# First norm applied behind the products, and four helper queues in another order, in a fused Trainium2 block kernel

## Chip, cores and metric

The kernel runs as one launch on one core of one Trainium2 chip. The metric is the device time of one launch in microseconds (us), the median over several runs; lower is better. The core has a matrix engine (TensorE, PE in the rows), a vector engine (VectorE, DVE), a scalar engine (ScalarE, ACT), GpSimd (POOL) and a queue of DMA issues on SyncE (SP); each works through its own instructions in the order written, and they wait for one another through semaphores only.

## The reference, cut to what matters

The whole network is computed for 256 tokens of width 1024: a gated linear recurrence layer, a key/value projection, a sliding-window attention layer, a feed-forward layer, a two-branch mixer, a second feed-forward layer and a final norm. The change touches the first layer and its surroundings:

```
h = rmsnorm(x, norm_g)                    # x * rsqrt(mean(x*x) + 1e-6) * g
u = h @ w_in                              # 1024 x 3072
xb, gate = u[..., :1536], u[..., 1536:]
xb = causal_depthwise_conv(xb, conv_w, conv_b)        # 4 taps over time
r = sigmoid(blocks(xb) @ wr + br)         # 16 blocks of 96
i = sigmoid(blocks(xb) @ wi + bi)
log_a = -8.0 * r * softplus(-lam)
a = exp(log_a)
b = sqrt(-expm1(2.0 * log_a)) * (i * xb)
hs = scan(a, b)                           # h[t] = a[t] h[t-1] + b[t]
x = x + (hs * silu(gate)) @ w_out
```

## The kernel before, in words

**Products.** Activations lie transposed, 128 channels on the partitions and 256 tokens along them, so the width 1024 is 8 tiles `k`. Each float32 product is made of three products of rounded parts: weight high part by activation high part, weight high by activation low, weight low by activation high (`passes`, L595). Weights come in chunks of 1 MB, each as two halves of 128x1024 numbers, into a double buffer `stage`. SP's queue issues the loads (L392); a load into a buffer waits until VectorE has finished with what lay in it. `hi(n)` on ScalarE rounds half `n` to `w_hi` (all ScalarE work is recorded at L1216), `lo(n)` on VectorE subtracts to give `w_lo` (L1729). Both go into a ring of four halves; PE frees a place (`ring_free`) when it has used a half. A half is 24 matmuls.

**First layer.** `a_w_in` is 12 chunks: `C_X` 0 to 5 give the convolved branch, `C_G` 6 to 11 the gate branch, one PSUM bank per chunk (256 channels by 256 tokens). Halves are numbered through all of them, with the block gates between: gate group g (0 to 3) has two smaller halves of 128x768, numbers 8 and 9, 12 and 13, 18 and 19, 22 and 23. Groups 0 and 1 follow chunks 3 and 4, groups 2 and 3 follow chunks 6 and 7. So halves 16 and 17 are chunk 6, 20 and 21 chunk 7, 24 and 25 chunk 8.

**What a convolved chunk c needs** when its products are done: `conv_b` (ScalarE, two instructions from the bank, last tap and bias), `conv` (VectorE, six `scalar_tensor_tensor`, the other three taps, bank and SBUF as sources, L1942), `xb_hi(c)` (ScalarE) and `xb_lo(c)` (VectorE, L1734). PE may write the bank of chunk c again when the convolution has read it (`conv_x`).

**What a gate group g needs**: its two halves; the convolved activations; and `stack(g)`, eight copies on POOL (L487) that gather the pieces of 96-wide blocks which straddle tiles. PE first runs 18 "main" matmuls, then 12 "rest" matmuls (L825 and L827) that read the stacked copies. Behind them ScalarE runs six tanh instructions, and `decay(g)` (six instructions, exponents); `decay` needs `lam_ready`, the last of some 15 tiny VectorE instructions (128x12) that compute softplus(-lam) by a series (L1883 to L1907). `lru_gated`, `lru_square`, `gate_out` and `decay_square` (POOL) follow.

**The start.** Both token halves of x are loaded, then chunk 0 of the weights. ScalarE and VectorE form the mean square of each token (squares summed along x), the root and its reciprocal; x is scaled by it (`rooted_x`, L1836), transposed a second time two tiles ahead of use (`turn_ahead`, L617), multiplied by the gain while it is split into `a_hi` (`normalised_hi`) and `a_lo` (L1841). Raw x is transposed too (L794) and copied to `xres` for the residual (`input_out`). `warm` (L783) are matmuls on constants ahead of the data.

**POOL's queue** holds, in this order: the gate weight pieces of groups 0 and 1 (L495, L503), those of groups 2 and 3, `stack(0)`, `stack(1)`, eight further pieces, 14 small loads for later layers (L507 to L519), `stack(2)`, a `decay_square`, `stack(3)`.

The order of work is written out by hand: each engine's program is a loop over the half number `n` with conditions in it. ScalarE's and VectorE's read, before:

```python
                if n - 1 in x_end:          # ScalarE
                    xb_hi(x_end[n - 1])
                if n not in x_end and n:
                    hi(n + 4)
                act.wait_ge(ring_free, n + 1)
                if n in x_end:
                    c = x_end[n]            # conv_b(c), then hi(n + 4)
```

## Time and profile before

| what | value |
|---|---|
| median of 3 runs | 785.8 us (785.65 to 786.15) |
| the profiled execution | 785.83 us |
| its span, first to last record | 783.9 us |
| PE busy | 775.7 us, 99% of the span, 5321 matmuls |
| VectorE busy | 585.7 us, 75% |
| ScalarE busy | 487.7 us, 62% |
| GpSimd busy | 107.1 us, 14% |

All rows come from the profiled execution. Starts are in us from the start of the span. In rows of a timeline the first number is the start, the second the time from the start of the first to the end of the last instruction of the row; in brackets stands how long the engine had been idle and for whom it waited. A row of one source line gives min/median/max duration in ns and the starts of the first and the last instruction. Instructions of one engine overlap a little, so the distance between two starts is shorter than a duration.

### The profile page before, as it was taken

How to read it: one execution, taken by the hardware profiler on the slowest of the kernel's cores; microseconds unless marked ns; L12 is line 12 of the kernel's file. 1: busy time of each engine (PE TensorE's matmuls, PEld its weight loads, DVE VectorE, ACT ScalarE, POOL GpSimd, SP SyncE). 2: the span in 40 equal slices, each digit the busy share in tenths (PEclk: the TensorE clock that was granted, in tenths of full speed). 3: DMA queues.
4: the chain of work that ended last, by engine and by line, in shares of the span. 5: the costliest groups of instructions: out<-in, count | busy, mean ns of one | idle time of the engine just before them, and what ended most of it. 6: DMA issues, size and time to landing. Idle time of an engine off the chain costs nothing.

```text
span 783.9 us, 14573 instructions
## 1 busy us (share of the span) xinstructions
PE 775.7 (99%) x5321; PEld 710.9 (91%) x5321; DVE 585.7 (75%) x892; ACT 487.7 (62%) x761; POOL 107.1 (14%) x195
## 2 busy tenths in 40 slices
PE   8999999999999999999999999999999999999997
PEld 7999999998998888888888899999999888888885
DVE  5998997978868887776459664796588887787443
ACT  7799947778675655554346565764656665555334
POOL 9697100157100000000000031000000000000000
PEclk9999999999999999999999999999999999999999
DMA  8663575634546766666665554445655676765651
GB/s 261 191 191 113 180 205 165 205 109 111 186 135 185 218 190 187 185 206 195 187 188 167 182 153 145 130 143 158 186 166 157 193 215 186 195 184 184 193 182 54
DMA packets 101557, 136.57 MB, mean 174 GB/s; under 512 B 5320, under 2 KB 86912, under 8 KB 101504
## 3 DMA queue, kind: packets, MB, share of 16 engines
q1 hardware_dynamic: 99232, 133.23, 56.4%
q0 software_dynamic: 2112, 2.54, 1.3%
q8 instruction: 35, 0.57, 0.3%
q14 instruction: 18, 0.15, 0.1%
q10 hardware_dynamic: 160, 0.07, 0.0%
HBM read 134.78 MB, written 1.05 MB: 173 GB/s over the span
## 4 chain that ended last, share of the span: by engine, by line
PE 96%; DVE 2%; ACT 1%; DMA 1%; issue 0%; SPq 0%; ACTq 0%
PE bank L595 34%; PE bank L658 21%; PE bank L660 11%; PE bank L603 8%; PE bank L704 8%; PE bank L751 5%; PE bank L752 3%; PE bank L945 1%; PE bank L927 1%; PE bank L952 1%; ACT acts L1216 1%; DMA arena<-x 1%; DVE w_lo L1729 1%; PE bank L955 0%; DVE acts L1767 0%; PE bank L827 0%
## 5 line engine op out<-in xcount | busy, mean ns | idle before, releaser
L1729 DVE TENSOR_TENSOR w_lo<-stage,w_hi 128x1024 fp32r<-128x1024 f32 x249 | 305.1, 1230 | 124.0 <-ACT w_hi L1216 123.4
L1216 ACT ACTIVATE w_hi<-stage 128x1024 fp32r<-128x1024 f32 (+1 forms) x251 | 262.4, 1051 | 117.6 <-PE bank L595 41.8
L595 PE MATMUL bank<-acts,w_hi 128*128 128x256 f32 x1520 | 277.3, 285 | 0.4 <-DVE acts L1841 0.3
L658 PE MATMUL bank<-acts,w_hi 128*128 128x512 f32 x704 | 244.8, 392 | 0.0
L595 PEld LDWEIGHTS bank<-acts,w_hi 128*128 128x128 f32 x1520 | 236.5, 192 | 2.7 <-issue 1.7
L595 PE MATMUL bank<-acts,w_lo 128*128 128x256 f32 x760 | 214.9, 283 | 0.0
L660 PE MATMUL bank<-acts,w_lo 128*128 128x256 f32 x704 | 197.2, 280 | 0.0
L658 PEld LDWEIGHTS bank<-acts,w_hi 128*128 128x128 f32 x704 | 131.7, 187 | 29.2
L595 PEld LDWEIGHTS bank<-acts,w_lo 128*128 128x128 f32 x760 | 145.7, 192 | 0.0
L660 PEld LDWEIGHTS bank<-acts,w_lo 128*128 128x128 f32 x704 | 133.1, 189 | 0.0
L1216 ACT ACTIVATE arena<-bank 128x512 f32<-128x512 f32 (+1 forms) x79 | 43.6, 561 | 63.7 <-PE bank L660 45.9
L603 PE MATMUL bank<-w_hi,acts 128*128 128x256 f32 (+1 forms) x320 | 71.8, 319 | 0.4 <-DVE w_lo L1729 0.4
L555 POOL TENSOR_SCALAR arena<-arena,rden 128x128 f32<-128x128 f32 (+1 forms) x44 | 23.4, 544 | 283.8 <-DVE rden L2108 283.2
L751 PE MATMUL bank<-acts,w_hi 128*128 (+1 forms) x176 | 61.1, 391 | 0.0
L1216 ACT ACTIVATE acts<-arena 128x512 fp32r<-128x512 f32 (+3 forms) x41 | 26.4, 644 | 52.7 <-DVE arena L2262 33.0
L1216 ACT ACTIVATE arena<-arena 128x512 f32<-128x512 f32 (+3 forms) x64 | 38.4, 605 | 29.7 <-DVE arena L2238 14.6
L603 PEld LDWEIGHTS bank<-w_hi,acts 128*128 128x128 f32 x320 | 52.2, 191 | 4.6 <-DVE w_lo L1729 0.8
L704 PE MATMUL bank<-w_hi,acts 128*128 128x512 f32 x176 | 54.4, 390 | 0.0
L603 PE MATMUL bank<-w_lo,acts 128*128 128x256 f32 (+1 forms) x160 | 50.5, 315 | 0.0
L752 PE MATMUL bank<-acts,w_lo 128*128 (+1 forms) x176 | 49.3, 280 | 0.0
L2230 DVE TENSOR_TENSOR arena<-arena,bank 128x512 f32<-128x512 f32 x44 | 30.2, 685 | 22.2 <-ACT arena L1216 22.2
L751 PEld LDWEIGHTS bank<-acts,w_hi 128*128 128x128 f32 x176 | 32.9, 187 | 7.2
(221 smaller groups left out, 809.4 us busy)
## 6 DMA issues: line engine op xcount, KB each, us to landing
stage<-ffn_w_gate SPq DMA_DIRECT2D x44, 512.0 KB, 4.3
stage<-ffn_w_up SPq DMA_DIRECT2D x44, 512.0 KB, 4.5
stage<-ffn_w_down SPq DMA_DIRECT2D x44, 512.0 KB, 3.6
stage<-w_in SPq DMA_DIRECT2D x40, 512.0 KB, 3.6
stage<-a_w_in SPq DMA_DIRECT2D x24, 512.0 KB, 4.5
stage<-b_w_in SPq DMA_DIRECT2D x16, 512.0 KB, 3.9
stage<-a_w_out SPq DMA_DIRECT2D x12, 512.0 KB, 3.7
stage<-b_w_out SPq DMA_DIRECT2D x8, 512.0 KB, 3.5
```

The source lines that it names most:

```text
L555: pool.tensor_scalar(s, s, rden[:, 2 * n + q:2 * n + q + 1], 1.0, ALU.mult, ALU.mult).then_inc(p_norm, 1)
L595: mm = pe.matmul(dst, w[:, slot, c:c + P], a[:, k, :] if isinstance(k, int) else a[:, bass.ds(k, 1), :], start=start and n == 0, stop=stop ...
L603: mm = pe.matmul(dst, a[:, k, tb * P:(tb + 1) * P], w[:, slot, c:c + n], start=start and i == 0, stop=stop and i == 2, skip_group_check=True)
L658: pe.matmul(two[p][:, m, :], w_hi[:, half % RING, c:c + P], wide(acts[:, k, :, :]), start=k == 0, stop=False, skip_group_check=True)
L660: mm = pe.matmul(two[p][:, m, 0:T], w_lo[:, half % RING, c:c + P], a_hi[:, k, :], start=False, stop=k == KD - 1, skip_group_check=True)
L704: mm = pe.matmul(token_bank(tb, h)[:, :], a[:, k, t], w[:, slot, c], start=False, stop=w is w_hi and a is a_hi, skip_group_check=True)
L751: pe.matmul(b[:, :], w_hi[:, half % RING, w], both, start=start, stop=False, skip_group_check=True)
L752: return pe.matmul(b[:, 0:T], w_lo[:, half % RING, w], high, start=False, stop=stop, skip_group_check=True)
L927: mm = pe.matmul(bank[score_bank(n + i)][:, c:c + w], q[r, t * T + c:t * T + c + P], k[r, 0:keys], start=True, stop=True)
L1216: return nc.scalar.activation(out_, in_, func, **kw)
L1729: dve.tensor_tensor(w_lo[:, n % RING, 0:w], src, w_hi[:, n % RING, 0:w].bitcast(F32), ALU.subtract)\
L2230: dve.tensor_tensor(y, y, two[ffn_two(n, j, u)][:, :, 0:T], ALU.add).then_inc(ff_add, 1)
```

## The change

1. x is loaded in halves of columns (channels 0 to 511, then 512 to 1023), with the first weight half between them. Raw x is transposed once, 16 transposes, into banks 0 to 3 and 6, 7 (`turned_x`); `a_hi` and `a_lo` are made from it with the gain alone. `rooted_x` and `turn_ahead` are gone. `WARM` goes from (8, 3) to (11, 2).
2. The squares are summed in four parts later on. The token factor is spread over the partitions by two matmuls inside chunk 1 (`first_roots`), copied to `spread`, and multiplied into each chunk's bank afterwards: `x_scale(c)` (VectorE, six times, result in SBUF at `x_unit`) for the convolved branch, and `gate_out(0..5)` for the gate branch, where 0 to 2 were plain copies before and 3 to 5 did not exist (`silu` read the bank).
3. `conv_b` and `conv` read `x_unit` in SBUF. PE waits for `x_scaled` of chunk c - 2 where it waited for `conv_x`. `gates(0)` waits for `x_ready` 4, now set by the last copy to `xres`, behind `conv_b(2)`.
4. ScalarE does `hi(n + 4)` ahead of `xb_hi` and ahead of `conv_b`; VectorE does `lo(n + 4)` ahead of `xb_lo` and ahead of `conv`.
5. The softplus series goes to POOL, ahead of `stack(0)`, 18 instructions in a chain (`decay_scale`); Abs and Exp stay on ScalarE, one sum and the reciprocal on VectorE.
6. Of the second pair's gate pieces 6 stay on POOL and 14 go to SP's queue, behind the loads of chunks 2, 3 and 4. The 14 small loads for later layers go from POOL to SP's queue, 11 behind the load of chunk 9 and 3 behind that of chunk 11.

```diff
-WARM = (8, 3)
+WARM = (11, 2)
...
-            for tb in range(TB):
-                sp.dma_start(x_tok[:, tb, :], xt[:, tb, :]).then_inc(x_in[tb], 16)
+            for j in range(2):
+                sp.dma_start(x_tok[:, :, 512 * j:512 * j + 512], xt[:, :, 512 * j:512 * j + 512]).then_inc(x_in[j], 16)
+                sp.dma_start(stage[:, 0, j, :].rearrange("p (b n) -> p b n", b=4), first[:, 4 * j:4 * j + 4, :])\
+                    .then_inc(stage_in[j], 16)
...
             for j in range(2, 6):
                 load(C_X + j, col(w_in, j), split(C_X + j - 2))
+                if j == 2:
+                    second_pieces()
+                elif j < 5:
+                    second_again(j - 3)
...
+            pieces(1, 0, 6)
+            decay_scale()
+            stack(0)
+            stack(1)
...
+            def first_roots():
+
+                pe.wait_ge(rstd_ready, 1)
+                pe.wait_ge(x_ready, 1)
                 for tb in range(TB):
-                    mm = pe.transpose(bank[5 + k % 3][:, tb * P:(tb + 1) * P], x_rst[:, tb, k * P:(k + 1) * P], ident)
-                mm.then_inc(xt_done, 1)
+                    mm = pe.matmul(bank[6][:, tb * P:(tb + 1) * P], n_rstd[:, tb:tb + 1].to_broadcast([P, P]),
+                                   ident, start=True, stop=True)
+                mm.then_inc(first_rb, 1)
...
                 if c >= 2:
-                    pe.wait_ge(conv_x, 2 * (c - 1))
-                col_chunk(C_X + c, 4 + c % 2, normed=0)
+                    pe.wait_ge(x_scaled, c - 1)
...
+                if n:
+                    hi(n + 4)
                 if n - 1 in x_end:
                     xb_hi(x_end[n - 1])
-                if n not in x_end and n:
-                    hi(n + 4)
                 act.wait_ge(ring_free, n + 1)
                 if n in x_end:
                     c = x_end[n]
-                    if c == 0:
-                        act.wait_ge(par_ready, 2)
+                    act.wait_ge(x_scaled, c + 1)
                     for m in range(2):
                         t = 2 * c + m
-                        f(tiles(XB + t), bank[4 + c % 2][:, m * T:(m + 1) * T], ACT.Identity,
+                        f(tiles(XB + t), x_unit(c)[:, m * T:(m + 1) * T], ACT.Identity,
...
                     if c == 0:
-                        input_out(2)
-                        input_out(3)
-                        hi(4)
-                    hi(n + 4)
+                        input_out(7)
+                    elif c < 3:
+                        input_out(2 * c - 2)
...
+            def x_scale(c):
+
+                dve.wait_ge(ring_free, half_of(C_X + c) + 2)
+                rooted(XU + 2 * (c % 2), 4 + c % 2).then_inc(x_scaled, 1)
...
                 if n - 1 in x_end:
+                    lo(n + 4)
                     xb_lo(x_end[n - 1])
...
                 if n in x_end:
                     c = x_end[n]
+                    x_scale(c)
...
+                    lo(n + 4)
...
-                            dve.scalar_tensor_tensor(x[:, tap:T], bank[4 + c % 2][:, m * T:(m + 1) * T - tap],
+                            dve.scalar_tensor_tensor(x[:, tap:T], x_unit(c)[:, m * T:(m + 1) * T - tap],
                                                      par_a[:, w:w + 1], x[:, tap:T], ALU.mult, ALU.add)\
```

How the queues change at three places.

VectorE around chunk 2 and gate group 0. `L1729` (now `L1823`) is `lo`, with `gate_st` of a gate group's half; `L1942` (now `L2022`) the convolution; `L1734` (now `L1828`) `xb_lo`; `L1913` `x_scale`. Before:

```order
L1734 TENSOR_TENSOR acts<-arena,acts 128x2x256 [waits xbh]
L1729 TENSOR_TENSOR w_lo<-gate_st,w_hi 128x768 [waits hi_done]
L1887 RECIPROCAL lam<-lam 128x12 [waits lam_step]
L1889 TENSOR_TENSOR lam<-lam 128x12 [waits lam_step]
L1942 SCALAR_TENSOR_TENSOR arena<-bank,par_a,arena 128x255 [waits conv_b]
L1942 SCALAR_TENSOR_TENSOR arena<-bank,par_a,arena 128x255
L1942 SCALAR_TENSOR_TENSOR arena<-bank,par_a,arena 128x254 [waits conv_s] x2
L1942 SCALAR_TENSOR_TENSOR arena<-bank,par_a,arena 128x253 [waits conv_s] x2
L1729 TENSOR_TENSOR w_lo<-gate_st,w_hi 128x768 [waits hi_done]
```

Now:

```order
L1823 TENSOR_TENSOR w_lo<-gate_st,w_hi 128x768 [waits hi_done]
L1828 TENSOR_TENSOR acts<-arena,acts 128x2x256 [waits xbh]
L1913 TENSOR_TENSOR arena<-bank,spread 128x512 [waits ring_free]
L1823 TENSOR_TENSOR w_lo<-gate_st,w_hi 128x768 [waits hi_done]
L2022 SCALAR_TENSOR_TENSOR arena<-arena,par_a 128x255 [waits conv_b]
L2022 SCALAR_TENSOR_TENSOR arena<-arena,par_a 128x255
L2022 SCALAR_TENSOR_TENSOR arena<-arena,par_a 128x254 [waits conv_s] x2
L2022 SCALAR_TENSOR_TENSOR arena<-arena,par_a 128x253 [waits conv_s] x2
```

Half 8 is now split ahead of `xb_lo(1)` and half 9 ahead of `conv(2)`, `x_scale(2)` stands between, and the convolution reads no bank.

ScalarE from gate group 1's tanh to gate group 2's halves. `lam` marks `decay`, `w_hi<-arena` the halves of group 2, `bank,par_a` with x5 tanh, two alone (or `arena,par_a` now) `conv_b`. Before:

```order
L1216 ACTIVATE arena<-bank,par_a 128x256 x5
L1216 ACTIVATE w_hi<-stage 128x1024 [waits ring_free,stage_in2]
L1216 ACTIVATE arena<-bank,par_a 128x256 [waits ring_free]
L1216 ACTIVATE arena<-bank,par_a 128x256
L1216 ACTIVATE w_hi<-stage 128x1024 [waits ring_free,stage_in3]
L1216 ACTIVATE arena<-arena,lam 128x256 [waits ri_sig,lam_ready]
L1216 ACTIVATE arena<-arena,lam 128x256 x5
L1216 ACTIVATE acts<-arena 128x2x256 [waits conv_x]
L1216 ACTIVATE w_hi<-stage 128x1024 [waits ring_free,stage_in0]
L1216 ACTIVATE w_hi<-stage 128x1024 [waits ring_free,stage_in1]
```

Now:

```order
L1304 ACTIVATE arena<-bank,par_a 128x256 x5
L1304 ACTIVATE w_hi<-stage 128x1024 [waits ring_free,stage_in2]
L1304 ACTIVATE w_hi<-stage 128x1024 [waits ring_free,stage_in3]
L1304 ACTIVATE arena<-arena,par_a 128x256 [waits x_scaled,ring_free]
L1304 ACTIVATE arena<-arena,par_a 128x256
L1304 ACTIVATE arena<-arena,lam 128x256 [waits ri_sig,lam_ready]
L1304 ACTIVATE arena<-arena,lam 128x256 x5
L1304 ACTIVATE w_hi<-stage 128x1024 [waits ring_free,stage_in0]
L1304 ACTIVATE acts<-arena 128x2x256 [waits conv_x]
L1304 ACTIVATE w_hi<-stage 128x1024 [waits ring_free,stage_in1]
```

Half 15 goes ahead of `conv_b(4)`, which now also waits for `x_scale(4)`; half 16 still stands behind `decay(0)` but ahead of `xb_hi(4)`.

POOL between its gate pieces and `stack(0)`. Before, `stack(0)` (L487) followed the last piece of gate_i:

```order
L495 DMA arena<-a_gate_i_w 64x2x96 x2
L495 DMA arena<-a_gate_i_w 32x2x96
L495 DMA arena<-a_gate_i_w 96x2x96
L487 CAST acts<-acts 32x256 [waits xbl]
L487 CAST acts<-acts 32x256 [waits stack_done] x3
L487 CAST acts<-acts 64x256 [waits stack_done] x4
```

Now the end of `decay_scale` stands there (an ISA row and the first 13 of its instructions are left out):

```order
L572 TENSOR_SCALAR lam<-lam 128x12 [waits lam_step]
L573 TENSOR_TENSOR lam<-lam 128x12 [waits lam_step]
L574 TENSOR_SCALAR lam<-lam 128x12 [waits lam_step]
L575 TENSOR_TENSOR lam<-lam 128x12 [waits lam_step]
L576 TENSOR_TENSOR lam<-lam 128x12 [waits lam_step]
L533 CAST acts<-acts 32x256 [waits xbl]
L533 CAST acts<-acts 32x256 [waits stack_done] x3
L533 CAST acts<-acts 64x256 [waits stack_done] x4
```

## Rows read from the trace of the kernel before

**Rows 1.** The page: busy time by engine.
```profile
PE 775.7 (99%) x5321; PEld 710.9 (91%) x5321; DVE 585.7 (75%) x892; ACT 487.7 (62%) x761; POOL 107.1 (14%) x195
```

**Rows 2.** Chain of waits that ended last, first 125 us: start, length, what.
```profile
9.96 0.98 PE bank L595 x6
...
17.91 19.66 PE bank L595 x162
37.57 0.12 PE bank L825
...
39.01 7.92 PE bank L595 x66
...
63.49 7.92 PE bank L595 x66
72.85 11.52 PE bank L595 x96
84.43 40.38 PE bank L595 x336
```

**Rows 3.** Timeline of PE and ScalarE, the start.
```profile
1.01 3.79 PE L783 MATMUL bank<-ones 128*128 128x128 f32 x16 [1.01 <-POOL half_pi L476]
5.23 1.97 PE L794 MATMUL bank<-con,arena 128*128 128x128 f32 x16
7.04 0.83 PE L783 MATMUL bank<-ones 128*128 128x128 f32 x6
7.79 0.63 ACT L1216 ACTIVATE w_hi<-stage 128x512 fp32r<-128x512 f32 x1 [0.40 <-DMA stage<-a_w_in]
17.63 0.25 PE L839 MATMUL bank<-con,rows_a 96*128 96x96 f32 x1
```

**Rows 4.** Line L775: a later norm's spread, the same form as `first_roots`.
```profile
L775 PE MATMUL bank<-con,n_rstd x8: 270/274/275, 145.8 to 425.9; 128*128 128x128 f32 x8
```

**Rows 5.** Timeline of VectorE, chunks 0 to 3.
```profile
19.48 2.42 DVE L1942 SCALAR_TENSOR_TENSOR arena<-bank,par_a,arena 128x255 f32<-128x255 f32 x6
21.82 2.35 DVE L1729 TENSOR_TENSOR w_lo<-stage,w_hi 128x1024 fp32r<-128x1024 f32 x2
24.08 0.68 DVE L1734 TENSOR_TENSOR acts<-arena,acts 128x512 fp32r<-128x512 f32 x1
30.79 0.95 DVE L1729 TENSOR_TENSOR w_lo<-gate_st,w_hi 128x768 fp32r<-128x768 f32 x1
31.66 0.22 DVE L1887 RECIPROCAL lam<-lam 128x12 f32<-128x12 f32 x1
```

**Rows 6.** Costliest groups by form: a bank times `spread`, in later norms.
```profile
L1819 DVE TENSOR_TENSOR arena<-bank,spread 128x512 f32<-128x512 f32 x14 | 9.6, 684 | 4.8 <-PE bank L595 4.8
```

**Rows 7.** Timeline of ScalarE, gate groups 1 and 2.
```profile
42.13 2.27 ACT L1216 ACTIVATE arena<-bank,par_a 128x256 f32<-128x256 f32 x6
44.27 1.09 ACT L1216 ACTIVATE w_hi<-stage 128x1024 fp32r<-128x1024 f32 x1
45.21 1.05 ACT L1216 ACTIVATE arena<-bank,par_a 128x256 f32<-128x256 f32 x2
46.11 1.10 ACT L1216 ACTIVATE w_hi<-stage 128x1024 fp32r<-128x1024 f32 x1
47.06 3.07 ACT L1216 ACTIVATE arena<-arena,lam 128x256 f32<-128x256 f32 x6
50.01 0.64 ACT L1216 ACTIVATE acts<-arena 128x512 fp32r<-128x512 f32 x1
```

**Rows 8.** Timeline of POOL: `stack(0)` and `stack(3)`.
```profile
30.94 5.13 POOL L487 CAST acts<-acts 32x256 fp32r<-32x256 f32 x8 [5.94 <-DVE acts L1734]
...
61.82 8.68 POOL L487 CAST acts<-acts 32x256 fp32r<-32x256 f32 x8 [0.68 <-POOL arena L525]
```

**Rows 9.** Line L487 on POOL at 32.2 to 33.5 (beside the convolution), then at 66.0 to 70.5.
```profile
L487 POOL CAST acts<-acts x4: 390/396/398, 32.1 to 33.4; 32x256 fp32r<-32x256 f32 x3, 64x256 fp32r<-64x256 f32 x1
...
L487 POOL CAST acts<-acts x4: 1001/1010/1271, 66.0 to 69.2; 64x256 fp32r<-64x256 f32 x4
```

**Rows 10.** Line L1729 on VectorE, 61.5 to 70.5, beside `stack(3)`.
```profile
L1729 DVE TENSOR_TENSOR w_lo<-stage,w_hi x3: 1212/1412/1415, 61.6 to 68.8; 128x1024 fp32r<-128x1024 f32 x3
L1729 DVE TENSOR_TENSOR w_lo<-arena,w_hi x2: 1003/1074/1146, 65.8 to 67.8; 128x768 fp32r<-128x768 f32 x2
```

**Rows 11.** Timeline of POOL, one small copy twice, in the attention layer.
```profile
154.38 0.19 POOL L560 COPY arena<-sink 128x1 f32<-128x1 f32 x1
...
155.12 1.18 POOL L560 COPY arena<-sink 128x1 f32<-128x1 f32 x1
```

**Rows 12.** DMA issues from 4 to 80 us: count, size, median us to landing.
```profile
stage<-a_w_in SPq DMA_DIRECT2D x22, 512.0 KB, 4.4
```

More of the change, by code:

```diff
@@ L409, in stream @@
                 j = 0
-                while j < n and chunk + j < C_G + 3:
-                    load(chunk + j, view(j), split(chunk + j - 2) if chunk + j >= 2 else None)
-                    j += 1
                 turns = (n - j) // 2
@@ new lines, in _ @@
+            for first, name in ((KV_G, "kv_norm_g"), (FIN_G, "final_norm_2")):
+                sp.dma_start(rows_b[first:first + KD, :], I[name].rearrange("(k p) -> k p", p=P))\
+                    .then_inc(rows_b_in, 16)
+            for h in range(2):
+                sp.dma_start(rows_b[K_G:K_G + 1, h * HD:(h + 1) * HD], I["k_norm_g"].rearrange("(o d) -> o d", o=1))\
+                    .then_inc(rows_b_in, 16)
+                sp.dma_start(rows_b[Q_G:Q_G + 1, h * HD:(h + 1) * HD], I["q_norm_g"]).then_inc(rows_b_in, 16)
@@ L450, in _ @@
+            for j in range(4, 6):
+                load(C_G + j, col(w_in, j + 6), split(C_G + j - 2))
+            sp.dma_start(con[:, P:N_CONST], I["constants"][:, P:N_CONST]).then_inc(con_in, 16)
+            sp.dma_start(pos[:, :], I["positions_2"].rearrange("o (b p) -> p (o b)", p=P),
+                         allow_slow_non_contiguous=True).then_inc(pos_in, 16)
+            sp.dma_start(sink[:, :], I["sinks"].to_broadcast([P, NQ])).then_inc(sink_in, 16)
             stream(C_AO, 6, lambda j: row(w_out, j))
@@ new lines, in first_chunk @@
+            def first_chunk():
+                for k in range(KD):
+                    h, kk = divmod(k, 4)
+                    if k == 0:
+                        pe.wait_ge(w_first_hi, 1)
+                        pe.wait_ge(xl_ready, 1)
+                        for m in range(2):
+                            for a in (a_hi, a_lo):
+                                pe.matmul(bank[4][:, m * T:(m + 1) * T], w_hi[:, 0, m * P:(m + 1) * P], a[:, 0, :],
+                                          start=m == 0 and a is a_hi, stop=False, skip_group_check=True)
+                        pe.wait_ge(w_first, 1)
+                        for m in range(2):
+                            pe.matmul(bank[4][:, m * T:(m + 1) * T], w_lo[:, 0, m * P:(m + 1) * P], a_hi[:, 0, :],
+                                      start=False, stop=False, skip_group_check=True)
+                        continue
+                    if kk == 0:
+                        pe.wait_ge(w_first, h + 1)
+                    if kk == 2:
+                        pe.wait_ge(w_done, h + 1)
+                    pe.wait_ge(xl_ready, k + 1)
+                    for m in range(2):
+                        mm = passes(bank[4][:, m * T:(m + 1) * T], h, kk * T + m * P, k, False, k == KD - 1)
+                    if kk == 3:
+                        mm.then_inc(ring_free, 1)
+                    if k == 4:
+                        pe.wait_ge(rows_a_in, 16 * 5)
+                        pe.transpose(bank[5][:, 0:ROWS_A], rows_a[:, :], con[0:ROWS_A, IDENT:IDENT + ROWS_A])\
+                            .then_inc(par_t, 1)
@@ L789, in _ @@
             pe.transpose(bank[7][:, 0:KD], rows_n[:, :], con[0:KD, IDENT:IDENT + KD]).then_inc(par_t, 1)
-            for tb in range(TB):
-                pe.wait_ge(x_in[tb], 16)
-                for m in range(KD):
-                    c = (m % 2) * T + tb * P
-                    mm = pe.transpose(bank[m // 2][:, c:c + P], x_tok[:, tb, m * P:(m + 1) * P], ident)
-                    if tb == 1 and m % 2:
-                        mm.then_inc(acc_done, 1)
+            pe.wait_ge(x_in[0], 16)
+            first_turns(0)
             warm(WARM[1])
-            turn_ahead(0)
-            turn_ahead(1)
+            pe.wait_ge(x_in[1], 16)
+            pe.wait_ge(par_ready, 1)
+            first_turns(4)
             def gates(g):
@@ L1857, in _, with first_weights @@
-            normalised_lo(2)
-            normalised_lo(3)
-            lo(1)
-            for k in range(4, KD):
-                normalised_lo(k)
+            def first_weights(h, part):
+                dve.wait_ge((w_first_hi, hi_done)[part], h + 1)
+                at = slice(part * 2 * T, (part + 1) * 2 * T)
+                dve.tensor_tensor(w_lo[:, h, at], stage[:, 0, h, at], w_hi[:, h, at].bitcast(F32), ALU.subtract)\
+                    .then_inc((w_first, w_done)[part], 1)
+            dve.wait_ge(x_in[0], 16)
@@ new lines, in _ @@
+            dve.wait_ge(ms_part_d, 2)
+            dve.tensor_tensor(n_ms[:, :], fin_ms[:, 0:2], fin_ms[:, 2:4], ALU.add).then_inc(ms_ready, 2)
+            dve.wait_ge(par_ready, 2)
+            root_inv(0)
+            lo(4)
+            dve.wait_ge(first_rb, 1)
+            dve.tensor_copy(spread[:, :], bank[6][:, 0:T]).then_inc(first_sb, 1)
+            dve.wait_ge(first_sb, 1)
+            def x_scale(c):
+                dve.wait_ge(ring_free, half_of(C_X + c) + 2)
+                rooted(XU + 2 * (c % 2), 4 + c % 2).then_inc(x_scaled, 1)
@@ L2001, in _ @@
             lo(30)
+            gate_out(3)
             lru_input(1)
@@ L2007, in _ @@
             lo(32)
+            gate_out(4)
             lru_scan(4)
@@ L2010, in _ @@
             lo(33)
+            gate_out(5)
             gated_h(1)
```

334 lines of the change are left out of this document (160 added, 174 removed).

## The prediction

> **What bounds the kernel now.** I read the busy times first: PE works 99% of the span, VectorE 75%, ScalarE 62% [rows 1]. So only two things can change the time: work on PE, and waits of PE. The chain of waits shows where those are. Before the first product at 9.96 PE does no product; from 17.91 to 124.8 it hardly stops: 162 matmuls in 19.66 us and 336 in 40.38 us are 0.12 us each [rows 2]. A half of 24 is thus 2.88 us, a chunk 5.76, a gate group 3.6 (2.16 main, 1.44 rest). Before, PE waits nowhere in chunks 1 to 12. The fixed points to compare with are the rest of group 0 at 37.57, chunk 4 at 39.01, half 20 at 63.49, chunk 8 at 72.85 [rows 2]. The gain can only come from the start, and it survives only if VectorE, ScalarE and POOL, which get more to do and another order, deliver earlier too.
>
> **A. The start: 2.6 us gained.** First, 22 warm matmuls instead of 16 (3.79 us, 0.24 each [rows 3]) last 5.2 us and end at 6.2. Eight transposes take 1.0 (16 in 1.97) and four warm ones 0.55 (6 in 0.83), together to 7.75, hidden behind the load of x's second half. That load is third on SP's queue, as the first weight half was, which was there at 7.79 [rows 3]. Eight more transposes take 1.0, so products begin at 8.85 instead of 9.96. Scaling, root and second transposes are no longer ahead of them. Chunk 0 takes 8 tiles of 6 matmuls, 8 x 0.72 = 5.76, plus the transpose of the parameters, 0.25 [rows 3]; chunk 1 starts at 14.85 instead of 17.91. Of this gain of 3.06 us, 1.1 come from the earlier start, and the rest from 12 transposes and the small gaps that stood between products. `first_roots` returns 0.5: two matmuls of 0.27 [rows 4]. Net 2.6. All further product work is the same.
>
> **B. VectorE up to gate group 0: 1.2 left.** The factor can be spread at about 18.95 (its square sums and the root stand between halves 2, 3 and 4). From there VectorE has no gap, start to start: spread copy 0.4, `x_scale(0)` 0.60, sum 0.1, half 5 1.14, reciprocal 0.16, `conv(0)` 2.34, ends 23.8. 1.14 and 2.34 are distances of starts (21.82 less 19.48, and half of 24.08 less 21.82 [rows 5]); 0.60 is the 0.68 of a bank-times-spread instruction less the same overlap [rows 6]. A chunk then costs 1.14 + 0.60 (`xb_lo`) + 0.60 (`x_scale`) + 1.14 + 2.34 = 5.8 us against PE's 5.76: before it was 5.2 plus the series. So VectorE is even with PE and never ahead. `conv(1)` ends at 29.6; half 8 (0.87) and `xb_lo(1)` 0.60 let `stack(0)` start at 31.1, before 30.94 [rows 8]: nothing gained there. `x_scale(2)` ends 31.7, `conv_b(2)` and the copies to `xres` behind it 33.5: `gates(0)` waits 0.9 for them (wanted at 32.6). Its main part ends 35.7, while `stack(0)`, taken at its 5.13 [rows 8], ends 36.4. Rest at 36.4 instead of 37.57.
>
> **C. ScalarE's order in group 1: 0.6 left.** PE would want half 16 at 36.4 + 1.44 + 5.76 + 3.6 + 5.76 = 52.95. `conv(3)` ends at 41.0; then ScalarE does `xb_hi(3)`, half 13, tanh 2.14, half 14 (to 45.5). VectorE splits half 14, scales chunk 4 (47.4), and only then `conv_b(4)` runs, to 48.4; before it was through at 46.1 [rows 7]. Behind it stands `decay(0)`, 2.96 [rows 7], then half 16: high part 52.3, low part 53.5. PE waits 0.55. The wait added to `conv_b` thus has `decay` queued behind it, and `decay` has the next half.
>
> **D. The same in group 2: 0.8 lost.** Half 20 is wanted at 53.5 + 5.76 + 3.6 = 62.9. `xb_hi(4)`, half 17, tanh, half 18 to 56.7; then `x_scale(5)` on VectorE to 58.3, `conv_b(5)` to 59.1, `decay(1)` to 62.1, half 20 63.1, low part 64.3. PE waits 1.4; before it began at 63.49.
>
> **E. Group 3: 1.1 lost.** `xb_lo(5)` now comes behind half 20, so `stack(3)` starts at 64.95. It took 8.68 with a start inside other work, and seven casts of 1.01 plus one of 0.4 are 7.4 [rows 8, 9]: ends 72.35, wanted at 64.3 + 5.76 + 2.16 = 72.2. 0.15 there and 0.15 at half 25.
>
> **F. POOL and VectorE hold each other up: 1.4 lost.** A cast takes 0.396 beside a convolution that reads a bank, and 1.01 beside `w_lo`, which reads two SBUF operands [rows 9]; those `w_lo` go from 1.212 to 1.412 and from 1.003 to 1.146 [rows 10]. Now the convolution has two SBUF sources. `stack(0)` and `stack(1)` run beside `conv(2)` and `conv(3)`, 12 instructions. Casts at one per convolution instruction still fit into about 5.1 us, but each instruction can be stretched by nothing to 0.20. I take 0.12, nearest to the shorter form. VectorE has no gap there, so it goes through: 12 x 0.12 = 1.4. (`conv(5)` has cover: ScalarE's `decay` is later.) Bounds: 0 to 2.4.
>
> The Trainium skill, "SBUF — State Buffer", section "SBUF: two separate sides", calls this an exclusive lock kept for a whole instruction, the other blocking fully. The slowed casts agree; the 0.2 on `w_lo`, half a cast, does not show a full block. By the page the term would be 12 x 0.4 = 4.8, a rival below.
>
> **G. Priced at nothing.** The 18 series instructions on POOL start at 21.5 and must be done by 31.1: 9.6 us, 0.53 each. A small copy took 0.19 free and 1.18 held up [rows 11]. Between 21.5 and 31.1 VectorE ends 18 instructions with two SBUF sources, so one gap for each: it just fits. Their cover is the wait for `xb_lo(1)`; gone, they cost one for one (third rival). The series leaves VectorE: some 15 instructions, counted in B. The 14 gate pieces on SP's queue stand between loads of 4.4 us to landing [rows 12], far ahead of halves 4 to 11; the small loads likewise. Bounds: nothing to 1 us if a half comes late. `gate_out` 3 to 5, three of 0.60, fall behind half 30, where VectorE has slack. Copies 0 to 2 become products of the same length.
>
> **Sum.** -2.6 at the start; -1.2 at group 0; -0.6 at half 16; +0.8 at half 20; +1.1 at chunk 8; with F +2.5. The profiled execution took 785.83 us, 1.9 more than its span, and equals the median 785.8. 785.8 + 2.5 = **788.3 us**. Bounds: F at 0 gives 786.9, at 2.4 789.3; lengths of VectorE's steps 3% longer add 1.2 more up to group 1, and the start may be off by 0.4: 790.8. About 0.2%, 1.6 us, is what a measurement can tell from no change: 784.2 to 787.4.
>
> **Rivals.**
> 1. *Faster.* The helpers keep up and the whole 2.6 stays: 783.2. For it: before, PE waits for no half in chunks 1 to 12, and ScalarE and VectorE are busy 62% and 75% over the whole [rows 1]. It needs half 20 ready at 60.9, 3.4 us before my walk. A walk over a hundred steps can be so wrong if one long step (tanh or `decay` behind `conv_b`) in truth lies beside another. Decides: a wait of PE at halves 16 and 20, or none. 0.22.
> 2. *No visible difference.* The walk holds, but the stretch of F is nothing, or the start gains a little more: 786.9, 784.2 to 787.4. 0.27.
> 3. *Clearly slower, series late.* POOL's chain is held up as the casts were, 1.0 each [rows 9]: 18 us, to 39.5, `stack(0)` to 44.6, PE's rest 7.0 us late, after which the helpers have caught up: 785.8 + 7.0 + 0.2 = 793.0. From 0.53 each it costs one for one. Against it: tiny instructions, and short convolution instructions leave many gaps. 0.05.
> 4. *Full lock.* 1.1 + 4.8: 791.7. 0.04. The Trainium skill's page named above gives this case.
> 5. The order does not do what it says, or loads come late behind the pieces: no single time. 0.02.
>
> **How the numbers follow.** Forecast case 0.40, 787.4 to 790.8, all slower by over 0.2%. Faster 0.22, same 0.27, slower 0.40 + 0.05 + 0.04 + 0.02 = 0.51. The range takes the forecast, the second rival and most of the first: 783.0 to 790.8; left out are rivals 3 to 5 and a corner of the first and of the forecast, 0.17. Both signs hold weight; the likeliest case alone is 787.4 to 790.8.
>
> **What would show it.** Right: first product near 8.85, chunk 1 near 14.9; `stack(0)` starting near 31.1; PE waits before `gates(0)` (0.9, on a copy to `xres`), on `stack(0)` (0.7), on halves 16 (0.5) and 20 (1.4), half 20 beginning at 64 or later; convolution instructions of 0.47 growing to about 0.6 beside casts. Wrong: `conv_b(4)` done by 46, half 20 before 62, no wait on `w_lo` between 45 and 65, or `stack(0)` starting before 29 or after 33. After half 30 the two should run alike; a loss there would be one I have not seen.

## The result and the profile after

The changed kernel takes **792.16 us** (792.11 to 792.55, 4 runs) against 785.84 us for the one before (785.65 to 786.15): ratio 1.0081, 95% interval 1.0069 to 1.0094. It is 6.3 us slower. The forecast was slower too, but by 2.5 us (788.3), and the range ended at 790.8. The profiled execution took 792.11 us, its span is 790.3 (before 783.9). Of all executions below one, of e15, ran at a mean granted clock of 0.753 and took 942.55 us; the medians are of the others.

PE's own work hardly changed: the page of the changed kernel has it busy for 776.1 us, before 775.7 [rows 1]. So 6.0 of the 6.4 us by which the span grew are time in which PE stood still. The timeline of PE in the changed kernel, the rows that begin a stretch and a few more; most rows between them are left out (in brackets the idle time before them and its releaser; L660 is a product, L676 a transpose of x, L915 a group's rest):

```profile
0.99 5.06 PE L877 MATMUL bank<-ones 128*128 128x128 f32 x22 [0.99 <-POOL half_pi L522]
...
7.21 0.61 PE L877 MATMUL bank<-ones 128*128 128x128 f32 x4
8.18 1.09 PE L676 MATMUL bank<-con,arena 128*128 128x128 f32 x8 [0.36 <-DMA arena<-x]
9.03 0.72 PE L690 MATMUL bank<-acts,w_hi 128*128 128x256 f32 x4
12.73 0.48 PE L660 MATMUL bank<-acts,w_hi 128*128 128x256 f32 x2
...
34.04 0.50 PE L660 MATMUL bank<-acts,w_hi 128*128 128x256 f32 x2 [1.20 <-ACT xres L1304]
38.42 0.39 PE L915 MATMUL bank<-acts,w_hi 128*128 128x256 f32 x1 [1.97 <-POOL acts L533]
49.83 0.47 PE L660 MATMUL bank<-acts,w_hi 128*128 128x256 f32 x2 [0.36 <-DVE w_lo L1823]
56.78 0.47 PE L660 MATMUL bank<-acts,w_hi 128*128 128x256 f32 x2 [0.97 <-DVE w_lo L1823]
67.99 0.47 PE L660 MATMUL bank<-acts,w_hi 128*128 128x256 f32 x2 [1.62 <-DVE w_lo L1823]
76.69 0.39 PE L915 MATMUL bank<-acts,w_hi 128*128 128x256 f32 x1 [0.55 <-POOL acts L533]
107.82 0.47 PE L660 MATMUL bank<-acts,w_hi 128*128 128x256 f32 x2 [0.21 <-DVE w_lo L1823]
```

Read it against the same points of the kernel before. [rows 2] gives them from the chain, whose rows of products behind chunk 1 lie 0.16 us later than the starts of the matmuls. Its timeline has the starts of the rest of group 0, of half 20 and of chunk 8:

```profile
37.41 0.28 PE L825 MATMUL bank<-acts,w_hi 128*128 128x256 f32 x1
...
63.33 0.40 PE L595 MATMUL bank<-acts,w_hi 128*128 128x256 f32 x2
...
72.69 0.40 PE L595 MATMUL bank<-acts,w_hi 128*128 128x256 f32 x2
```

The first product is 0.9 us early (9.03 for 9.96). Tile 5 of chunk 0 at 12.73 puts chunk 1 near 14.9, 3 us early. Then the waits come in the places the prediction named: gate group 0, `stack(0)`, halves 16 and 20, `stack(3)`, and two small ones in places that it did not name (49.83, half 14, and 107.82). The rest of group 0 is 1.0 late, half 20 4.7, chunk 8 (78.22) 5.5. The last 0.8 us of the loss come behind chunk 8: at the next wait that both kernels have, 149.07 (before 142.78), PE is 6.3 late. The places are mostly right, the sizes are not.

The helpers, from the timeline of VectorE. L2022 is the convolution, L1823 `lo`, L1828 `xb_lo`, L1913 `x_scale`:

```profile
24.09 1.22 DVE L1823 TENSOR_TENSOR w_lo<-stage,w_hi 128x1024 fp32r<-128x1024 f32 x1
25.23 0.69 DVE L1828 TENSOR_TENSOR acts<-arena,acts 128x512 fp32r<-128x512 f32 x1
25.83 0.68 DVE L1913 TENSOR_TENSOR arena<-bank,spread 128x512 f32<-128x512 f32 x1
...
27.74 2.45 DVE L2022 SCALAR_TENSOR_TENSOR arena<-arena,par_a 128x255 f32<-128x255 f32 x6
...
33.48 3.29 DVE L2022 SCALAR_TENSOR_TENSOR arena<-arena,par_a 128x255 f32<-128x255 f32 x6 [0.36 <-ACT arena L1304]
40.74 3.16 DVE L2022 SCALAR_TENSOR_TENSOR arena<-arena,par_a 128x255 f32<-128x255 f32 x6
...
62.55 4.16 DVE L2022 SCALAR_TENSOR_TENSOR arena<-arena,par_a 128x255 f32<-128x255 f32 x6 [0.30 <-ACT arena L1304]
```

Convolutions of 2.42 [rows 5] have become 3.29, 3.16 and 4.16 where POOL works beside them, and stay 2.45 where it does only tiny work or none (27.74, 51.51). POOL's timeline, the same kernel (L572 is a step of the series, L533 a stack's copy, L590 `decay_square`):

```profile
23.94 2.03 POOL L572 TENSOR_SCALAR lam<-lam 128x12 f32<-128x12 f32 x1
33.43 4.94 POOL L533 CAST acts<-acts 32x256 fp32r<-32x256 f32 x8
64.12 1.52 POOL L590 TENSOR_TENSOR arena<-arena 128x768 f32<-128x768 f32 x1
68.57 8.06 POOL L533 CAST acts<-acts 32x256 fp32r<-32x256 f32 x8 [2.93 <-issue]
```

`stack(0)` starts at 33.43, not at 31.1: the series was in its way until then. The row at 23.94 is one of its steps, which took 2.03 us where most take 0.3.

### The profile page after: what moved, and what is told of

Same layout as the page of the kernel before. It is cut to its first block, busy times and chain, and to the rows that moved or that the text cites. A ratio compares the mean times of both kernels' runs of the same rounds, so it can differ in the third digit from the quotient of the medians.

```text
span 790.3 us, 14567 instructions
## 1 busy us (share of the span) xinstructions
PE 776.1 (98%) x5313; PEld 711.0 (90%) x5313; DVE 591.5 (75%) x887; ACT 487.5 (62%) x761; POOL 102.0 (13%) x185
## 4 chain that ended last, share of the span: by engine, by line
PE 84%; DVE 6%; ACT 3%; POOL 3%; issue 2%; DMA 1%; SPq 0%; DVEq 0%; ACTq 0%; POOLq 0%
PE bank L660 24%; PE bank L752 20%; PE bank L754 11%; PE bank L668 8%; PE bank L798 8%; PE bank L845 5%; PE bank L846 3%; DVE w_lo L1823 2%; POOL acts L533 2%; ACT arena L1304 1%; ACT w_hi L1304 1%; PE bank L1033 1%; PE bank L1015 1%; PE bank L1040 1%; DMA stage<-a_w_in 1%
## 5 line engine op out<-in xcount | busy, mean ns | idle before, releaser
L1823 DVE TENSOR_TENSOR w_lo<-stage,w_hi 128x1024 fp32r<-128x1024 f32 x248 | 304.0, 1230 | 126.0 <-ACT w_hi L1304 125.4
L660 PE MATMUL bank<-acts,w_hi 128*128 128x256 f32 x1516 | 276.6, 285 | 4.5 <-DVE w_lo L1823 3.2
L660 PEld LDWEIGHTS bank<-acts,w_hi 128*128 128x128 f32 x1516 | 235.8, 192 | 7.1 <-issue 5.3
L660 PE MATMUL bank<-acts,w_lo 128*128 128x256 f32 x758 | 214.3, 283 | 0.0
L660 PEld LDWEIGHTS bank<-acts,w_lo 128*128 128x128 f32 x758 | 145.2, 192 | 0.0
L1304 ACT ACTIVATE arena<-bank 128x512 f32<-128x512 f32 (+1 forms) x76 | 41.8, 560 | 62.7 <-PE bank L754 46.0
L1304 ACT ACTIVATE acts<-arena 128x512 fp32r<-128x512 f32 (+3 forms) x41 | 26.3, 641 | 53.1 <-DVE arena L2335 33.0
```

Of the source, the lines that this page charges most:

```text
L660: mm = pe.matmul(dst, w[:, slot, c:c + P], a[:, k, :] if isinstance(k, int) else a[:, bass.ds(k, 1), :], start=start and n == 0, stop=stop ...
L1304: return nc.scalar.activation(out_, in_, func, **kw)
L1823: dve.tensor_tensor(w_lo[:, n % RING, 0:w], src, w_hi[:, n % RING, 0:w].bitcast(F32), ALU.subtract)\
```

## The experiments

Two theories stood at first. **Q**: VectorE's queue (with ScalarE's `decay` in it) is the bound from chunk 0 to half 20, and waits of PE only take one another's place. **P**: POOL's late `stack(0)` goes through to the end. Beside them: the new orders are at fault; the shared access to SBUF is; the loads are. Each run's time is a median that stands beside one of the kernel before, 785.75 to 785.87.

### The series: e1 and e6

e1 puts all of it behind both stacks:

```diff
-            decay_scale()
             stack(0)
             stack(1)
+            pool.wait_ge(stack_done, 2 * len(STACK))
+            decay_scale()
+            pool.wait_ge(lam_ready, 1)
```

> The changed kernel with the softplus series on POOL behind stack(0) and stack(1) instead of ahead of them, nothing else. Theory Q (VectorE's queue): VectorE has no gap from chunk 0 to half 11, so an earlier stack(0) only moves PE's wait from the stacked copies (1.97 us) to halves 14, 16 and 20; 791.5 to 792.2. Theory P (POOL): the series makes stack(0) 2.3 us later than my walk had it and this goes through to the end; 789.7 to 790.5. Both: stack(0) begins near 31.7 instead of 33.4.

Measured 793.87 us, slower than the changed kernel, outside both ranges. `stack(0)` did begin earlier (31.95), but the run answered another question: the series ran from 44.1 to 53.1, and `decay(0)` now waited for it, as ScalarE's timeline of e1 shows:

```profile
53.13 3.07 ACT L1306 ACTIVATE arena<-arena,lam 128x256 f32<-128x256 f32 x6 [1.80 <-POOL lam L576]
```

e6 puts only the last six steps behind `stack(0)`:

> The changed kernel with the softplus series cut in two: the last six of its instructions on POOL come behind stack(0) instead of ahead of it, and are done before decay(0) asks for them. This is the test that e1 was meant to be, without e1's wait of decay(0) for the series. Theory Q (VectorE's chain is the bound, PE's waits only take one another's place): stack(0) begins near 31.7, the wait for it shrinks from 1.97 to 0.2 to 0.5, the waits at halves 14 and 16 grow by as much; 791.7 to 792.3. Theory P (the late stack goes through): 790.2 to 790.7.

Measured 792.16 us, the same as the changed kernel to the last digit. `stack(0)` began at 31.84 and PE's wait for it was gone; waits of 0.91 and 0.28 us at halves 12 and 13 stood in its place. P falls, and Q's claim that waits only change places is shown for this wait.

### The orders: e2, e5 and e7

e2 moves `decay` behind `hi(n + 4)`, e7 moves `input_out` ahead of the wait for `x_scaled`, e5 puts both old orders back.

> The changed kernel with ScalarE's high parts of halves 16, 20 and 25 ahead of decay(0), decay(1) and decay(2), nothing else. Theory Q with the order as its second part: PE's waits on half 16 (0.97 us) and half 20 (1.62 us) shrink, the first to nothing, the second to what the stretched convolution of chunk 5 leaves; 1.2 to 2 us faster than the changed kernel, 790.2 to 791.0. Rival: the delayed decay makes decay_square, stack(3) and the group 3 rest later and gives it back; 791.9 to 792.5.

> The changed kernel with the copies to xres ahead of conv_b on ScalarE instead of behind it, so that gates(0) need not wait for conv_b(2). Theory Q: the wait of 1.2 us before gate group 0 shrinks to 0.3, and the one for stack(0) grows by the same; 791.9 to 792.4. Rival (each wait of PE counts for itself): 791.0 to 791.4.

> The changed kernel with both hand-written orders as they were before the change (conv_b and xb_hi ahead of hi; conv and xb_lo ahead of lo). Theory Q: conv_b(4) and conv_b(5) come 1 to 2 us earlier, decay and halves 16 and 20 with them, but the halves just before arrive later and stand in PE's way, since VectorE has no slack; between 790.5 and 793. Rival (the new order alone makes the loss): 787 to 789.

Measured: e2 791.88, e7 793.24, e5 797.74. e2 comes out as its rival said: 0.3 us for an expected 1.2 to 2, and its interval (1.0069 to 1.0097) does not tell it from the changed kernel. The wait at half 20 stayed (1.65, at 67.73). Those at halves 14 and 16 are gone from its profiled execution, but that is mostly not the edit's doing, as the clock paragraph below shows. e7 was to do nothing and cost 1.1 us, outside both of its ranges; its trace points to the clock. e5 lies outside both of its ranges too, and shows that the new orders are no fault: without them the change would cost 12 us, as VectorE's halves then stand in PE's way (8.9 us of waits for `w_lo`, seven of them).

e7's wait did move as Q says: 3.62 us in one piece before the rest of group 0. What followed is in the windows of e7 (the last three columns are granted clock, DMA share, GB/s):

```profile
34.00:38.00 4.00, 1.12 (x10) 0.91 (x8) 4.00 (x7) 1.54 (x3) 3.56 (x8) 0.92 0.00 0
38.00:42.00 4.00, 3.26 (x15) 3.27 (x16) 3.59 (x6) 2.45 (x4) 3.20 (x5) 0.50 0.43 133
42.00:46.00 4.00, 4.00 (x27) 4.00 (x27) 4.00 (x7) 1.40 (x4) 2.10 (x5) 0.72 0.46 131
46.00:50.00 4.00, 4.00 (x36) 4.00 (x35) 1.83 (x3) 4.00 (x9) 0.00 (x0) 1.00 0.02 4
```

Behind the wait the granted clock is 0.50, that is 1.2 instead of 2.4 GHz, for four microseconds and part of the next four: 15 matmuls where 27 should fit. In the changed kernel's profiled execution the two waits, 1.20 and 1.97, did not bring it down (1.00 in the window 35 to 60); in e2's and e3's, with almost the same waits, it was 0.83 in 35 to 45.

What such a fall costs at the end depends on what waits behind it. Where PE has hardly a further wait it cost some 2 us: of e15's executions, two took 787.01 and 787.53 us with a mean clock of 0.999, three 789.14 to 789.21 with 0.997. Where VectorE is the bound it cost nothing. e18 (below) is the changed kernel with 14 loads moved. The window 38 to 42 of the changed kernel, then of e18, then e18's half 20:

```profile
38.00:42.00 4.00, 3.58 (x30) 3.58 (x31) 3.90 (x7) 2.21 (x4) 3.20 (x5) 1.00 0.51 142
```

```profile
38.00:42.00 4.00, 3.54 (x18) 3.54 (x19) 3.91 (x7) 2.25 (x4) 3.20 (x5) 0.61 0.49 136
```

```profile
68.05 0.47 PE L660 MATMUL bank<-acts,w_hi 128*128 128x256 f32 x2 [1.63 <-DVE w_lo L1823]
```

PE fell 1.5 us behind by the rest of group 1 (49.39 for 47.87), the waits at halves 14 and 16 shrank by as much, and half 20 began at 68.05 for 67.99, released by the same `lo` of VectorE. That is the plainest evidence for Q in the record. It also means that e2's missing waits at 14 and 16 prove little, since e18 without e2's edit lacks them as well.

### The shared access: e3

`x_scale` of chunks 2, 3 and 5 writes into a PSUM bank that is free just then:

```diff
         def x_unit(c):
 
+            if c in (2, 3, 5):
+                return bank[0 if c == 4 else 6][:, :]
             return tiles(XU + 2 * (c % 2), 2)
...
+                if g >= 1:
+                    pe.wait_ge(conv_x, 2 * (g + 3) if g < 3 else 12)
```

> The changed kernel with x_scale of chunks 2, 3 and 5 writing into a free PSUM bank, so that conv_b and the convolution read a bank again, with waits that guard the bank. Theory Q with the shared access as its first part: convolutions beside the copies go back from 3.2 to 2.45 us (and 4.16 of chunk 5), the copies to 0.4 us, and of this 1.7 to 2.6 us reach the end; 789.6 to 790.5. Rival (the stretch is covered by ScalarE's decay): under 0.5 us, 791.7 or more.

Measured **789.83 us** (ratio 1.0053, 1.0040 to 1.0067), 2.3 below the changed kernel and inside Q's range. In the profiled executions 2.2 of it are there by the rest of group 3 (74.52 for 76.69). VectorE in e3, the convolutions of chunks 2, 3 and 5:

```profile
33.49 2.43 DVE L2030 SCALAR_TENSOR_TENSOR arena<-bank,par_a,arena 128x255 f32<-128x255 f32 x6 [0.29 <-ACT arena L1308]
39.41 2.43 DVE L2030 SCALAR_TENSOR_TENSOR arena<-bank,par_a,arena 128x255 f32<-128x255 f32 x6
60.81 2.43 DVE L2030 SCALAR_TENSOR_TENSOR arena<-bank,par_a,arena 128x255 f32<-128x255 f32 x6 [0.23 <-ACT arena L1308]
```

All are back at 2.43. Line L2022 of the changed kernel at 33 to 37, the same at 62 to 67, and L2030 of e3 at 33 to 37:

```profile
L2022 DVE SCALAR_TENSOR_TENSOR arena<-arena,par_a x6: 608/611/616, 33.5 to 36.2; 128x255 f32<-128x255 f32 x2, 128x254 f32<-128x254 f32 x2, 128x253 f32<-128x253 f32 x2
```

```profile
L2022 DVE SCALAR_TENSOR_TENSOR arena<-arena,par_a x6: 469/614/1683, 62.6 to 66.2; 128x255 f32<-128x255 f32 x2, 128x254 f32<-128x254 f32 x2, 128x253 f32<-128x253 f32 x2
```

```profile
L2030 DVE SCALAR_TENSOR_TENSOR arena<-bank,par_a,arena x6: 472/473/482, 33.5 to 35.4; 128x255 f32<-128x255 f32 x2, 128x254 f32<-128x254 f32 x2, 128x253 f32<-128x253 f32 x2
```

0.14 us per instruction beside copies (0.611 for 0.473; the prediction took 0.12), and one of 1.68 (at 64.24) beside `decay_square`, which has 1.52 itself and began first (64.12). The Trainium skill ("SBUF — State Buffer", section "SBUF: two separate sides") says that whoever starts first keeps the shared access for its whole instruction; the 1.68 agrees, while a copy of 0.39 costs 0.14, less than its own length.

### Both together: e8, e9, e11, e12

> The changed kernel with four edits together: series split (as in e6), copies first (as in e7), high parts of halves 16, 20 and 25 ahead of decay (as in e2), and the convolution of all six chunks from a PSUM bank (e3 had three of them). Theory Q: with VectorE no longer held up by POOL, each remaining wait has its own cause and the edits now add: no waits at halves 14, 16 and 20, under 1 us at gate group 0; 2 to 3 us faster than e3 with 789.8, so 786.8 to 787.8. Rival (VectorE's six x_scale instructions are the rest of the loss and cannot be hidden): 788.8 to 789.8.

> As e8, but with ScalarE's high parts behind decay as in the changed kernel. If the order before decay counts once VectorE is free: 0.5 to 1.5 us above e8. If it doesn't, as e2's 0.3 us suggests: within 0.3 us of e8.

Measured 789.39 and 790.01. No wait was left at halves 14 to 20 in e8, and still it beats e3 by 0.4 us only. That is in the rival's range, but the trace does not show the rival's cause: everything had gathered into one wait of 2.91 us for `stack(0)`, with a granted clock of 0.65 from 38 to 42 behind it. The 0.6 us between e8 and e9 lie within their intervals (1.0036 to 1.0063, 1.0039 to 1.0066), so the order before `decay` is not shown to count.

> As e8, with xb_lo(1) ahead of half 8 on VectorE again and the last part of the series behind stack(1). In e8 PE waited once, 2.91 us for stack(0), after which its granted clock was low for some 4 us. With stack(0) started 0.9 us earlier its last copy should no longer stand under the pair of half 10 and xb_lo(2), which held it for 2.03 us. Theory Q: wait for stack(0) under 0.7 us, no low clock, up to 1.5 us of waits at halves 12 to 14 in their place; 785.0 to 787.0. Rival (the wait only moves on): 788.5 to 789.5.

> As e11, but with the convolution reading SBUF as in the changed kernel. The difference to e11 is the cost of the shared access with the best order: convolutions 0.8 us longer beside copies, copies held up. Theory Q: 2 to 3.5 us above e11. Rival (order and copies were the whole loss): within 0.5 us of e11.

Measured 790.29 and 794.11, both outside what was expected. In e11 `stack(0)` did not start earlier than in e8 (32.12 for 31.93), but its copies took 4.80 us instead of 5.99. That took the wait for it down to 1.22 and the low clock away, and five waits took their place (0.58 at half 14, 1.04 and 0.55 at halves 20 and 21, 0.43, 0.21). Q again. The 3.8 us between e11 and e12 are the shared access together with what followed it, a low clock of 0.68 at 70 to 75 in e12 among it; the two are not separated.

### What the start can give at all: e10, e13, e15, e16

These leave the six `x_scale` out, so that the first norm's factor is missing in the convolved branch (e10; the others rotate the banks):

```diff
-            return tiles(XU + 2 * (c % 2), 2)
+            return bank[4 + c % 2][:, :]
...
-                    x_scale(c)
```

> The changed kernel without the six x_scale instructions: the first norm's factor is left out of the convolved branch, and the convolution reads the product's bank as before the change (PE waits for conv_x again). Everything else, the new start and both orders included, is as changed. Theory Q (VectorE's 3.6 us of x_scale ahead of half 14, which it has no gap for, eat the start's gain): PE waits under 1 us up to chunk 8 and the gain of the start shows, 783.5 to 785.5. Rival (the orders, the copies to xres or the series keep it slow even so): 787 or more.

> e10 again (the six x_scale instructions left out, so the convolved branch misses the norm's factor, and the convolution from the product's bank), now with the product banks rotated over 4, 5 and 6 so that chunk 2 need not wait for the convolution of chunk 0. In e10 that one wait was 2.87 us and PE's granted clock fell behind it; from chunk 3 to chunk 8 PE waited for nothing. Theory Q (x_scale is what VectorE has no time for): the start's gain shows whole, less first_roots and the slower load: 783.2 to 785.0. Rival (the new start itself, its loads and first_roots, gives no gain): 785.9 to 788.

> e13 with e11's order of the helpers: xb_lo(1) ahead of half 8, the last part of the series behind stack(1), copies to xres first, high parts ahead of decay. The six x_scale instructions are left out (the convolved branch misses the norm's factor); beside that and the product banks it is e11 with 790.3. In e13 PE waited 0.52 for a copy and 1.80 for stack(0), with a low clock behind it. Theory Q: these go, PE waits for almost nothing up to chunk 8, 784.0 to 785.6; the distance to e11 is what x_scale costs, 4.5 to 6 us. Rival (loads that land late behind the gate pieces on SP's queue are now the bound): 786.0 to 787.5 with waits of ScalarE for stage of over 2 us.

Measured 789.40, 787.04 and 789.14. e10's number is a wait of 2.87 us for chunk 0's bank and a clock of 0.83 (25 to 35) after it. e13 had no such wait and missed its 783.2 to 785.0 all the same; e15 missed too. In part that is the clock again: of e13's executions the two with a mean clock of 1.000 took 786.08 and 786.52 us, the four with 0.996 or 0.997 took 787.51 to 788.65.

So leaving out `x_scale` gives back 5.1 of the 6.3 us, more than any other edit. With the instruction go ScalarE's wait for it and the convolution's SBUF source; these runs do not price the three apart. But the start's gain does not appear even then, and Q in the form that promised it falls. The waits of ScalarE in e15, 8 to 60 us, name one further suspect:

```profile
ACT acts L1318 <- DVE arena L2038: 6.3, 4, 2.1
ACT w_hi L1318 <- DMA stage<-a_w_in: 1.9, 3, 0.9
```

`stack(0)` began at 32.0 with `x_scale` gone, as in e6 and e8 with it (31.84, 31.93). The loads are late. DMA engines are busy the whole stretch: in the changed kernel's windows (share is the last but one column) at 9 to 35 us (before: 0.85),

```profile
9.00:35.00 26.00, 24.80 (x208) 24.59 (x207) 24.02 (x47) 21.26 (x39) 24.23 (x45) 1.00 0.97 258
```

and a stage load issued at 10 to 30 us takes 6.4 us to land where it took 4.6 before. In between stand the 14 gate pieces; SP's queue in the changed kernel:

```profile
12.71 3.54 SPq L463 DMA_DIRECT2D arena<-a_gate_i_w  x6
17.34 3.48 SPq L468 DMA_DIRECT2D arena<-a_gate_r_w  x4
22.19 2.35 SPq L468 DMA_DIRECT2D arena<-a_gate_i_w  x4
```

> e13 (no x_scale, rotated banks; the convolved branch misses the norm's factor) with the 14 gate pieces of the second pair on SP's queue behind the load of chunk 5 and later instead of behind chunks 2 to 4, the series split and copies first. In e13 and e15 ScalarE waited 1.9 to 2.4 us for stage loads and VectorE's convolution of chunk 1 began no earlier than with x_scale. Theory L (loads are the second bound, right behind VectorE): stack(0) begins near 30.5 instead of 32.0, the wait for it under 1 us, no low clock; 784.5 to 786.3. Rival (something else holds conv(1)): as e15, 787 to 789.

Measured **786.10 us** (ratio 1.0004, 0.9995 to 1.0013), inside theory L's range: ScalarE's wait for loads fell to 0.2, and convolution 1 started at 27.59 instead of e15's 28.05. But two of L's signs missed: `stack(0)` began at 31.63, not near 30.5, and PE waited 1.72 for it, not under 1. And most of the distance to e15 and e13 can be clock, which did not fall in e16's profiled execution before PE's last product; at a full clock e13 took 786.1 to 786.5 as well. What the traces give the loads is the 0.5 us of convolution 1.

Even so e16 is no faster than before. By the rest of group 3 it is 0.45 us ahead (70.80 for 71.25), as the wait for `stack(0)` has eaten most of the start's gain, and behind chunk 8, where `gate_out` 3 to 5 stand, it loses the rest: 143.12 for 142.78.

> e8 (the four edits; nothing left out) with the 14 gate pieces late on SP's queue. If VectorE is the bound with x_scale and the loads only behind it: within 0.5 us of e8, 788.9 to 789.8. If the loads hold it up as much: 787.0 to 788.5.

> The changed kernel with the 14 gate pieces late on SP's queue and nothing else. Theory Q: VectorE has no gap there, so nothing, 791.8 to 792.4. Theory L alone: 790 to 791.5.

Measured 789.21 and 792.25: with `x_scale` in place the late loads cost nothing that can be told. VectorE is the first bound, the loads lie behind it. e18 also shows how much of the lateness comes from the pieces: stage loads issued at 20 to 30 us land after 4.7 us instead of 6.6, those issued at 10 to 20 still take 7.1 (6.4 in the changed kernel, 4.7 before), and why is open. e17 has the lowest time of those that compute the reference, 3.4 us slower than the kernel before.

### After chunk 8: e14

> The changed kernel without gate_out 3, 4 and 5: silu of these chunks reads the product's bank as before the change, so half of the gate branch misses the norm's factor. It measures the term that the prediction set at nothing. PE's last 1.0 us of loss comes after chunk 8 began. If these three instructions are it: 791.1 to 791.5. If they are hidden: 791.9 to 792.3.

Measured 791.55 us, 0.6 below the changed kernel; PE has no wait from 80 to 130 us, where the changed kernel had 0.2. The intervals of the two overlap (1.0060 to 1.0087 and 1.0069 to 1.0094), so 0.6 is likely, not certain. In the profiled executions 0.3 us of the difference are there before chunk 8 (rest of group 3 at 76.41 for 76.69), where the edit changes nothing; behind it stand 0.5 (148.33 for 149.07).

## Why the prediction was right and wrong

The direction, most places of the waits and the main mechanism were right: VectorE is the bound, and what is added to it goes through to PE. The step that failed is term F, the price of the shared access: 1.4 us in the sum, with `conv(5)` called covered, and 2.3 us measured by e3, where `conv(5)` alone was held 1.7 us longer. Beside it the time of `gate_out` 3 to 5, put at nothing, is likely some 0.5 (e14), and the hand-offs in the walk, also at nothing, came to 0.4 to 0.7.

- **A, the start: right.** 8.85 for 9.03 measured, chunk 1 at 14.85 for about 14.9. The loads' landing (7.8 for 8.2) was the difference.
- **B, VectorE up to group 0: order right, POOL wrong.** `conv(1)` was put at 27.3 and came at 27.74, `conv(2)` at 32.8 and came at 33.48: 0.4 to 0.7 us of hand-offs that the walk set at nothing, 0.25 of it before its first step (19.20 for 18.95). `stack(0)` at 31.1 came at 33.43. The step "one gap for each: it just fits" failed: a series step can be held over two VectorE instructions. That took PE's wait from 0.7 to 1.97, but e6 shows that it is worth nothing at the end. The series took 11.5 us for the 9.6 it was given (21.94 to 33.48).
- **C and D, halves 16 and 20: mechanism right, size off.** Forecast waits 0.55 and 1.4, measured 0.97 and 1.62, but 3.3 and 3.7 us later than the walk had them (53.5 and 64.3). Of this the sum had 1.4 as term F.
- **E: right in kind.** `stack(3)` took 8.06 us for 7.4, and the wait was 0.55 for 0.15.
- **F: the term that was mis-sized.** 12 instructions at 0.12 gave 1.4 us. The unit was nearly right (0.14), the count was not: `w_lo` and `xb_lo` beside the copies stretch too (1.42 and 0.88 at 36.7 and 38.0), and chunk 5, which the text called covered by `decay`, ran 4.16 us, 1.7 more than free, mostly because POOL's `decay_square` falls on it. It had no cover: the `lo` that released half 20 followed it without a pause (66.63). e3 measures 2.3 us for the three chunks.
- **G: `gate_out` 3 to 5 at nothing: likely wrong by some 0.5** (e14). VectorE has no slack there: from 80 to 110 us it is busy 29.97 of 30.00, and it was busy 29.19 in the kernel before, so that trace showed it already. The pieces on SP's queue at nothing: right at the end (e18), though they do make the loads of 20 to 30 us late.
- **Small slips in the sum.** The fixed points from the chain lie 0.16 us too late, which hides 0.16 of loss. The steps in B add up to 23.7, not 23.8, and the upper bound to 790.9, not 790.8.
- Miss: 792.2 less 788.3 is 3.9. Measured by an edit are 0.9 more for F, and with less certainty 0.5 for G; hand-offs before `conv(2)` 0.7 and `stack(3)` with its wait 0.6 are read from the trace, 0.2 is the chain's offset; 1.0 stays unassigned. The clock is not in it: in the changed kernel's profiled execution it was 1.00 up to PE's last product.
- **The rivals.** The faster one needed half 20 at 60.9; it began at 67.99, so it is dead, and even e16, without `x_scale`, gets there only at 62.8. The full lock (791.7) came nearest in time, by luck: it took 0.4 us for each convolution instruction and 4.8 in all, measured were 0.14 and 2.3. The late series (793.0) is not far off either, and its reason did not hold: `stack(0)` began 2.3 us behind the walk, not 8.4 (at 39.5), and e6 shows that this costs nothing.

## What to carry to other kernels

An earlier start is worth what the slowest helper chain behind it can follow: walk that chain with its hand-offs, and look at DMA share too, since the next bound may lie close behind. Moving a pass "behind the products" put 0.6 us per chunk on an engine that had 5.2 of 5.76 us to do already. Before an operand goes from PSUM to SBUF, count every VectorE instruction in that stretch that has two SBUF sources while GpSimd works, those of other chunks and GpSimd's longest instruction included. And when a wait of PE is removed and the time stays, look where it went before removing the next: three edits here (e6, e7 and e11 on top of e8) each removed or halved their wait and were worth nothing or less. Nor does a wait that is missing from one trace prove that an edit removed it: look at the granted clock ahead of it first.
